# Norm of the recurrence's keys in quarters: sums on four quarters of TensorE's columns, spread from four quarters of its rows

## The reference

```python
kk = heads(k * k_k).astype(jnp.float32)
kk = kk / jnp.maximum(jnp.sqrt(jnp.sum(kk * kk, axis=-1, keepdims=True)), 1e-12)
k = k * (1 + (a - 1) * k_a)
r_h, k_h, v_h = heads(r), heads(k), heads(v)
y = wkv7_scan(r_h, heads(decay), k_h, v_h, -kk, kk * heads(a).astype(jnp.float32))
```

## Time and profile before

| what | value |
|---|---|
| median of three runs | 828.59 us (827.99 to 830.95) |
| the profiled execution's own time | 829.7 us |
| its span, first to last instruction | 827.7 us |
| TensorE busy | 776.6 us, 94% of the span |
| mean granted TensorE clock | 0.966 of full speed |

### The profile page before, as it was taken

How to read it: one execution, slowest core, us unless ns; L and a number is a source line. 1 busy time by engine, 2 the same in 40 slices (tenths; PEclk the granted TensorE clock), 3 DMA queues, 4 the chain that set the end, 5 groups by cost and what they waited for, 6 DMA issues and landing times.

```text
span 827.7 us, 18045 instructions
## 1 busy us (share of the span) xinstructions
PE 776.6 (94%) x7577; PEld 726.4 (88%) x7577; DVE 526.0 (64%) x745; ACT 376.0 (45%) x577; POOL 73.0 (9%) x50
## 2 busy tenths in 40 slices
PE   7999997898869999999999999988889999999997
PEld 6987886897649999999999989875569999999997
DVE  3986875767543877774455774477836877764441
ACT  5675543121434544443444433437857444443331
POOL 0000005280130000000000010003420000000000
PEclk9999998989988999999999999977999999999999
DMA  9753330000112499756555543330004656565551
GB/s 297 234 157 102 102 102 2 4 3 14 42 52 78 145 243 235 206 182 210 189 185 178 158 148 103 102 102 1 1 1 153 182 178 198 179 203 184 191 159 51
DMA packets 110779, 108.74 MB, mean 131 GB/s; under 512 B 7120, under 2 KB 109776, under 8 KB 110592
## 3 DMA queue, kind: packets, MB, share of 16 engines
q1 hardware_dynamic: 110720, 107.88, 43.3%
HBM read 106.82 MB, written 1.05 MB: 130 GB/s over the span
## 4 chain that ended last, share of the span: by engine, by line
PE 84%; DVE 9%; ACT 4%; POOL 1%; issue 1%; DMA 1%; ACTq 0%; SPq 0%; DVEq 0%; POOLq 0%
PE ps L440 21%; PE ps L441 21%; PE ps L442 21%; PE ps L641 4%; ACT SB L1389 2%; DVE Gs L1626 1%; PE ps L779 1%; PE ps L535 1%; PE ps L861 1%; DVE SB L1938 1%; PE ps L979 1%; DVE nmx L1943 1%; PE ps L1001 1%; ACT PT L1400 1%; PE ps L470 1%
## 5 line engine op out<-in xcount | busy, mean ns | idle before, releaser
L1441 DVE TENSOR_TENSOR wlo<-raw,whi 128x1024 fp32r<-128x1024 f32 x188 | 225.1, 1221 | 103.6 <-ACT whi L1056 101.5
L440 PE MATMUL ps<-xh,whi 128*128 128x256 f32 x896 | 255.5, 285 | 0.0
L442 PE MATMUL ps<-xh,wlo 128*128 128x256 f32 x896 | 253.8, 283 | 0.0
L441 PE MATMUL ps<-xl,whi 128*128 128x256 f32 x896 | 253.6, 283 | 0.0
L1056 ACT ACTIVATE whi<-raw 128x1024 fp32r<-128x1024 f32 x124 | 130.4, 1058 | 151.1 <-PE ps L442 150.3
L440 PEld LDWEIGHTS ps<-xh,whi 128*128 128x128 f32 x896 | 170.0, 190 | 4.3 <-issue 3.4
L441 PEld LDWEIGHTS ps<-xl,whi 128*128 128x128 f32 x896 | 169.4, 189 | 0.3 <-issue 0.2
L442 PEld LDWEIGHTS ps<-xh,wlo 128*128 128x128 f32 x896 | 169.6, 189 | 0.0
L442 PE MATMUL ps<-hh,wlo 128*128 128x256 f32 x512 | 145.0, 283 | 0.0
L441 PE MATMUL ps<-hl,whi 128*128 128x256 f32 x512 | 144.7, 283 | 0.0
L440 PE MATMUL ps<-hh,whi 128*128 128x256 f32 x512 | 144.0, 281 | 0.0
(11 more groups left out here) (281 smaller groups left out, 1008.0 us busy)
## 6 DMA issues: line engine op xcount, KB each, us to landing
raw<-in_mlp_w SPq DMA_DIRECT2D x128, 512.0 KB, 3.7
raw<-in_rwkv_w_in SPq DMA_DIRECT2D x24, 512.0 KB, 4.9
raw<-in_nsa_w_in SPq DMA_DIRECT2D x20, 512.0 KB, 3.7
raw<-in_rwkv_w_out SPq DMA_DIRECT2D x8, 512.0 KB, 3.4
raw<-in_nsa_w_out SPq DMA_DIRECT2D x8, 512.0 KB, 4.5
cw<-in_nsa_cmp_w SPq DMA_DIRECT2D x4, 512.0 KB, 9.5
cst<-in_consts SPq DMA_DIRECT2D x1, 1039.0 KB, 10.6
xtok<-in_x SPq DMA_DIRECT2D x2, 512.0 KB, 4.4
```

The lines of the kernel that those rows point to most:

```text
L440: mm(o, wh, hi[:, kk, :], start=(kk == 0), stop=False)
L441: mm(o, wh, lo[:, kk, :], start=False, stop=False)
L442: last = mm(o, wl, hi[:, kk, :], start=False, stop=(kk == ktiles - 1))
L1441: v.tensor_tensor(wlo[:, slot, :], raw[:, slot, :], whi[:, slot, :].bitcast(f32), ALU.subtract)\
```

## The change

The 256 tokens are cut into four quarters of C = 64. For the sums, quarter i of the tokens is written to PSUM rows 32i to 32i+31, that is, by quarter i of the array's columns; the weight is 32 columns wide (two heads and 30 columns of zeros), so `hsel` in the constants grows by 16 columns. Root, maximum and reciprocal then work on 128 rows by 64 tokens in place of 16 by 256. For the spread, quarter i is read from rows 32i to 32i+31, by quarter i of the array's rows, and written to PSUM bank 4+i; so `spread` is repeated in four quarters of the partitions, and its load is 128 rows in place of 16. DVE's multiplication reads the banks in the new order. Each of the 8 products becomes 4.

```diff
-            for k in range(FT):
-                last = mm(ps[0:H, 6, 0:T], hsel(k), sq2[:, k, :], start=(k == 0), stop=(k == FT - 1))
-            last.then_inc(sem("kk_pe"), 1)
+            quarter_sums(6, lambda k: sq2[:, k, :], range(FT)).then_inc(sem("kk_pe"), 1)
...
-                    for k in range(FT):
-                        last = mm(ps[:, 4 + k // 2, (k % 2) * T:(k % 2 + 1) * T], hspread(k), kkr[:, 1, :],
-                                  start=True, stop=True)
-                    last.then_inc(sem("kk_pe"), 1)
+                    quarter_spread((4, 5, 6, 7), kkr[:, 1, :], range(FT)).then_inc(sem("kk_pe"), 1)
...
+            def quarter_sums(bank, x, tiles):
+                for k in tiles:
+                    w = cc("hsel")[:, H - 2 - 2 * k:3 * H - 2 - 2 * k]
+                    for i in range(4):
+                        last = mm(ps[32 * i:32 * i + 32, bank, 0:C], w, x(k)[:, C * i:C * i + C],
+                                  start=(k == tiles[0]), stop=(k == tiles[-1]))
+                return last
+            def quarter_spread(banks, rows, tiles):
+                for j, k in enumerate(tiles):
+                    for i in range(4):
+                        last = mm(ps[:, banks[i], j * C:(j + 1) * C], spread[32 * i:32 * i + 32, k * P:(k + 1) * P],
+                                  rows[32 * i:32 * i + 32, :], start=True, stop=True)
+                return last
...
-            A(kkr[:, 0, :], ps[0:H, 6, 0:T], ACT.Sqrt).then_inc(sem("kk_root"), 1)
+            A(kkr[:, 0, :], ps[:, 6, 0:C], ACT.Sqrt).then_inc(sem("kk_root"), 1)
...
-            v.tensor_tensor(KK[:, :, :].rearrange("p (b k) t -> p b (k t)", b=4), KK[:, :, :].rearrange("p (b k) t -> p b (k t)", b=4),
-                            ps[:, 4:8, :], ALU.mult).then_inc(sem("kkn_used"), 1)
+            kq = KK[:, :, :].rearrange("p k (i n) -> p i k n", n=C)
+            v.tensor_tensor(kq, kq, ps[:, 4:8, :].rearrange("p i (k n) -> p i k n", n=C), ALU.mult).then_inc(sem("kkn_used"), 1)
...
-    spread = place("spread", [H, D + FT + P], misc + 8320)
+    spread = place("spread", [P, D + FT + P], misc + 8320)
...
-        "hsel": np.arange(2 * H - 2)[None, :] == (H - 2 + i // HD)[:, None],
+        "hsel": np.arange(3 * H - 2)[None, :] == (H - 2 + i // HD)[:, None],
```

More of the change, by code:

```diff
@@ L96 @@
 for _n, _w in (("ident", P), ("mean", P), ("pair", P), ("center", P), ("gmask", 2 * C), ("lmask16", C), ("lmask32", C),
-               ("lmask64", C), ("eye64", C), ("hsel", 2 * H - 2), ("chunk", T),
+               ("lmask64", C), ("eye64", C), ("hsel", 3 * H - 2), ("chunk", T),
                ("dist", P * TT * (TT + 1) // 2), ("adc", TT * H * 16), ("unit", P), ("shift", P), ("last", 2)):
@@ L172, in rwkv_nsa_trunk @@
     E3 = Sg
-    kkr = place("kkr", [H, 2, T], misc + 4224)
+    kkr = place("kkr", [P, 2, C], misc + 4224)
     AR = place("AR", [P, FT, NCH, 2, C], off(7))
@@ L491, in hspread @@
             def hspread(k):
-                return spread[:, k * P:(k + 1) * P]
+                return spread[0:H, k * P:(k + 1) * P]
+            def quarter_sums(bank, x, tiles):
[11 more added lines that the diff above has]
+                return last
             pe.wait_ge(sem("xd_out"), 4)
@@ L728, in gn_spread @@
                 pe.wait_ge(sem("y_rstd"), c + 1)
-                mm(ps[:, 7, :], spread[:, D + FT:], rsb[:, :, :], start=True, stop=True).then_inc(sem("rstd_pe"), 1)
+                mm(ps[:, 7, :], spread[0:H, D + FT:], rsb[:, :, :], start=True, stop=True).then_inc(sem("rstd_pe"), 1)
             def xs_values(c):
@@ L1688, in gn_rstd @@
                 v.tensor_tensor(rsb[:, :, :], rst[:, 0:C].unsqueeze(1).broadcast_to([H, FT, C]),
-                                spread[:, D:D + FT].unsqueeze(2).broadcast_to([H, FT, C]), ALU.mult).then_inc(sem("y_rstd"), 1)
+                                spread[0:H, D:D + FT].unsqueeze(2).broadcast_to([H, FT, C]), ALU.mult).then_inc(sem("y_rstd"), 1)
             def gn_scale(c):
@@ L2070 @@
     aps["consts"] = nc.dram_tensor("in_consts", consts.shape, mybir.dt.float32, kind="ExternalInput").ap()
-    n = np.arange(H)[:, None]
+    n = np.arange(P)[:, None] % 32
     spread = np.concatenate([np.arange(D)[None, :] // HD == n, np.arange(FT)[None, :] == n // 2,
-                             np.arange(P)[None, :] // HD == n % 2], 1).astype(np.float32)
+                             (np.arange(P)[None, :] // HD == n % 2) & (n < H)], 1).astype(np.float32)
     arrays["in_spread"] = spread
```

## The result

| | median us | runs |
|---|---|---|
| before | 829.77 | 4 (827.99 to 834.41) |
| changed | 800.49 | 4 (799.21 to 801.13) |

The account below looks back on a forecast made before the run. TensorE, busy for 776.6 of 827.7 us, was taken as the bound; sums 1.59, spread 1.80 and clock 1.65 made 5.0 us, so 823.6 us from a median of 828.59, within 821.0 to 827.8.

Parts of the forecast that it names:

- the larger load: DMA of the wider `spread` and `hsel`: no cost, unit 8 with 0.8 us in hand; uncovered, up to 1.9 us.
- these two links: Sums (3.45 us) and spread (3.65 us) on the PE chain: time taken from them comes off the end.
- The sums: Key norm's sums as 64 records at 29 ns: 1.86 us in place of 3.45, a gain of 1.59.
- the floor of 29 ns: Pace taken for each quarter record of the sums, the shortest that the rows show for any matmul.
- less than 29 ns: Rival on the sums: four run at once, 1.0 us in place of 1.86, time 822.7 us; chance 0.11.
- The spread: Key norm's spread with loads overlapping in four row groups: 1.86 us in place of 3.65, a gain of 1.80.
- the rival with pairs: Only two row groups overlap in loads: spread stays at 3.7 us, time 827.0 us; chance 0.14.
- the slower one: Rival: quarter loads run one behind the other, spread 7.3 us, sums 4.0 us, time 832.8 us; chance 0.03.
- The clock: Behind the spread, in V's third group: no fall of TensorE's clock to 0.50, a gain of 1.65 us.
- my doubt whether each run has it: Rival: the clock's gain is missing since the median run had no fall, or falls move: 825.2 us; chance 0.24.
- The sum: Gains of 1.59, 1.80 and 1.65 us together: 5.0 us, giving 823.6 us for a median.
- Who is late next: At L577 and L583 behind the spread: nothing new waits, by 1.0 us.

Follow-up runs that it names:

- l5: Kernel before with 64 bytes left free behind the constants, repeated with more rounds: 807.88 us in 6 runs, ratio 0.9765.
- l2: Changed kernel with 64 bytes left free behind the constants, operands 128 bytes above their place before: 827.98 us in 10 runs, ratio 0.9978.
- l4: Kernel before with 128 bytes left free behind the constants: 832.77 us in 10 runs, ratio 1.0052.
- q1: Changed kernel with 64 bytes left free behind the constants, only the sums in quarters, the spread as before: 830.56 us in 10 runs.
- l1: Kernel before with 64 bytes left free behind the constants, no instruction changed: 812.76 us in 4 runs, ratio 0.9798.
- l3: Kernel before with everything 64 bytes higher, the weights' ring too: 828.99 us in 10 runs, ratio 1.0004.
- x1: Kernel before, own layout, without most of the weights' split behind the first four units (8 of 1024 columns): 825.49 us in 4 runs, ratio 0.9927.
- x2: Kernel before without most of the weights' split, with 64 bytes left free behind the constants: 806.32 us in 2 runs, ratio 0.9708.
- p1: Changed kernel with 128 bytes left free behind the constants, operands 192 bytes above their place before: 811.74 us in two runs, ratio 0.9815.
- p2: Changed kernel with 64 bytes left free ahead of the split weights (whi and wlo): 803.57 us in two runs, ratio 0.9716.

## Why the prediction was wrong

The forecast was 823.6 us, within 821.0 to 827.8; 800.49 came out.

- **The step that failed** is in the part on the larger load: "`hsel` adds 8 KB to a load of 1039 KB, 0.03 us at that rate." I priced the wider constants as a DMA and not as a shift of all that is placed behind them. The place alone takes the kernel before from 828.35 to 807.88 (l5), 20.5 us. At a place 0 apart the changed kernel is at 827.98 (l2), where the kernel before is at 832.77 (l4).
- "time taken from these two links comes off the end": right, but it treated the rest of PE's time as fixed. The chain held the hint: V's second group has 48 matmuls in 5.75 us, 120 ns each, for 256 columns each, which at 2.4 GHz are 107 ns. I used that pace to price the clock and did not ask what the other 13 ns were. The same trace holds the comparison, in V's third group at the granted clock of 0.50 (1.2 GHz):

```profile
108.83 0.41 PE L441 MATMUL ps<-xl,whi 128*128 128x256 f32 x1
...
111.39 0.41 PE L441 MATMUL ps<-xl,whi 128*128 128x256 f32 x1
```

  From the one to the other are 12 matmuls, 213 ns each, which is 256 columns at 1.2 GHz with nothing over. At 64 apart the matmuls at this clock are 213 ns apart too (l5). So the excess of 7 to 13 ns stands only at the full clock.
- **The sums**: forecast 1.59 us, measured 2.57. The mechanism was right, the floor of 29 ns wrong. L501's 64 records start within 1.3 us:

```profile
L501 PE MATMUL ps<-sq,cst x64: 218/219/245, 80.4 to 81.7; 128*32 128x64 f32 x64
```

  In the chain 58 take 0.89 us, 15 ns each: all four groups of columns run at once. From the first of the sums to V's first matmul it is 3.55 us in l4 and 1.41 in l2, a factor of 2.5, where I had written less than two. That is the rival "less than 29 ns", which I gave 0.11. The 25 ns which the Trainium skill ("TensorEngine Tiling (Array Packing)", Instruction Overhead) led me to estimate for the overhead is no floor here either. The other part of the 2.57 us, 0.43, lies ahead of that: the sums begin that much sooner behind the gate's first matmul. Six of their records start ahead of the gate's last one, which writes only the first 32 rows of PSUM.
- **The spread**: forecast 1.86 us, in the chain 1.94, 30 ns for a record. Loads of 128 columns into four groups of rows overlap (114 ns for one, as in the earlier trace rows); the rival with pairs would have shown 3.7, the slower one 7.3.
- **The clock**: forecast 1.65 us. In the changed kernel:

```profile
100.26:102.20 1.94, 1.94 (x65) 1.87 (x65) 1.94 (x3) 1.92 (x4) 0.00 (x0) 1.00 0.00 0
102.20:107.90 5.70, 5.70 (x53) 5.70 (x50) 5.31 (x4) 2.46 (x2) 0.00 (x0) 1.00 0.29 92
```

  No fall. It stands behind the spread, or begins within it (l5, q1), in all eight traces with 16 rows (before, l1, l3, l4, l5, q1, x1, x2) and in none of the eight with quarters or full rows, so my doubt whether each run has it was unfounded. Spread and clock together: forecast 3.45, measured 3.19.
- **The sum** of the change's own parts, 5.0 us: 5.76 on the path up to L577 and 4.8 in the medians of l4 and l2, at one and the same place.
- **Who is late next**: nobody, as forecast. The multiplication ends at 107.02 and L591 begins at 107.77, 0.75 us in hand where I had 1.0. DVE's reciprocal takes what L1686 took in the earlier trace rows, and the new order of L1615 costs nothing:

```profile
85.62 0.55 DVE L1588 RECIPROCAL kkr<-kkr 128x64 f32<-128x64 f32 x1
...
104.74 2.28 DVE L1615 TENSOR_TENSOR KK<-KK,ps 128x2048 f32<-128x2048 f32 x1
```

- **The larger load** cost nothing at unit 8: ACT takes it at 35.65 with no idle time before it.

```profile
26.75 1.06 ACT L1070 ACTIVATE whi<-raw 128x1024 fp32r<-128x1024 f32 x1 [2.57 <-DMA raw<-in_rwkv_w_in]
29.00 1.06 ACT L1070 ACTIVATE whi<-raw 128x1024 fp32r<-128x1024 f32 x1 [1.19 <-DMA raw<-in_rwkv_w_in]
...
35.65 2.00 ACT L1070 ACTIVATE whi<-raw 128x1024 fp32r<-128x1024 f32 x2
```

  The row at 35.65 is units 8 and 9. The waits for a DMA in the first two rows are for units 4 and 5, ahead of `spread` in the queue; l1, with the small load, has 3.1 us of them too.

**What stays open.** What picks one of the paces at a given place (113.3 or 117.8 at 64 apart, 118.6 or 120.0 at 0), and so why the changed kernel was at 800 us in seven of ten runs and near 809 in three. Only the profiled execution of each run has a trace, and those of the changed kernel were both quick. But both paces stand in the changed kernel's own trace, in V's second group and then in its third:

```profile
L441 PE MATMUL ps<-xl,whi x16: 280/281/282, 94.6 to 99.9; 128*128 128x256 f32 x16
L441 PE MATMUL ps<-xl,whi x16: 276/276/287, 102.4 to 107.5; 128*128 128x256 f32 x16
```

These are 45 matmuls from first to last, 117.8 and 113.3 ns each: the pace holds through a stage and can differ in the next. Each MLP has 1536 three-pass matmuls, and in p1 the whole first MLP runs at the slower pace. That is 1536 x 4.5 ns = 7 us, an estimate near the step from 801 to 809; no trace of a run at 809 is there to show that this is the step. That TensorE's two reads meet is what is left over after x1 and p2; no run shows the meeting itself. No kernel tried was better than the changed one.

## What to carry to other kernels

When a diff changes the size of a tile, look at everything placed behind it: here 64 bytes in the place of the operands were worth four times the change that caused them. Where TensorE is the bound, hold the time between its matmuls against columns over clock before calling its time fixed, and try a few distances between the buffers of weights and of moving operands; and when such a shift rides along with a change, time the change at two places with the same shift, or its own worth can't be read. Small matmuls that use few rows or columns of the array can be worth quartering: here four ran at once in both places, and behind the spread the clock stayed up.

## What the runs showed of the hardware that was not expected

- Three-pass matmuls of 256 columns with loads of 128 columns between them start 113.3 ns apart when weights and moving operands lie 64 bytes apart modulo 128, 118.6 to 120.0 at 0 and 118.3 to 118.4 at 96, with no wait and at a clock of 1.00. At 64 some stages run at 117.8, within one execution. At a clock of 0.50 they start 213 ns apart, 256 columns at 1.2 GHz, with no such excess.
- Four matmuls in four groups of columns (128*32, 64 moving) take 61 ns together (0.89 us for 58), four in four groups of rows with loads of 128 columns 121 ns (1.94 us for 16 such sets).
- The spread's matmuls on 16 rows (3.65 us) were followed by a clock of 0.50 for 3.4 to 6.8 us in eight of eight traces, although PE never paused; the same matmuls with 112 rows of zeros beside them were not (one trace).
